# Sub keys folded into the query weights on the chip, and a mixer in three PSUM banks with its SSD branch ahead of the level loop

## Chip, cores and metric

The kernel runs on one core of one Trainium2 chip. The time is device time of one execution in microseconds (us). The core's engines are PE (TensorE, matmuls and transposes, its weight loads shown as PEld), DVE (VectorE), ACT (ScalarE), POOL (GpSimd, which here issues the gathers) and SP (SyncE, which issues most loads); each has a queue of its own and works through it in order. They meet through semaphores. Sixteen DMA engines move the data. PSUM has eight banks of 512 fp32 values in each of 128 partitions.

## What is computed

One block over 1024 tokens of width 1024, in fp32:

```
x   = x + mixer(rmsnorm(x))          # SSD branch (8 heads x 64) and gated DeltaNet, "GDN" (4 heads x 128)
h   = rmsnorm(x) * norm_ffn_w
q   = (h @ w_q)                      # 16 lists (8 heads x 2 halves) of 128
s   = q . sub_keys                   # 16 lists of 128 scores
s1, s2 -> top 16 each -> 50 candidate sums -> top 16 of them   # 128 experts a token
y   = sum_k gate_k * gelu(h . u_tab[id_k]) * v_tab[id_k]
out = rmsnorm(x + y) * norm_final_w
```

The mixer's GDN part needs the inverse of a unit triangular matrix in each tile; the kernel builds it in seven levels (block sizes 1 to 64). Both tables, u and v, have 16384 rows of 4 KB.

## The kernel before

**Stages.** The front stage (`front_stage`, lines 194 on) normalises x, multiplies by w_in, convolves, and stores the results to scratch memory; near its end SyncE loads w_out and w_q, a slice of each (lines 288 and 289) behind each store. The tile stage (`tile_stage`, lines 533 on) takes the 1024 tokens in eight tiles of 128. For a tile it runs the mixer, the query product, and the two selections that give 128 picks for each token; then the expert part gathers a row of u for each of 128 picks (items "U": one gather of 128 rows, 512 KB, and one DVE product against h at L1180) and the rows of v (items "V": one gather for each token and two products on PE at L838).

**Rounds.** The expert part of tile e runs in the same round as the mixer of tile e+1. A round takes the loop body `body(m, e)`: `body(0, None)` is tile 0's mixer with no experts; `body(1, 0)` has tile 0's first half of experts; six full rounds follow, in which the first part interleaves this tile's U items with the previous tile's remaining 60 V items, and the last part is 68 V items; two bodies without a mixer end the program.

**Order.** Every engine's queue is written by the same two lists: the steps of the mixer and scoring (`steps`), and a fixed `SEQUENCE` of expert items. Between steps stands `share()`, and the n-th call emits the items up to `SHARE_ENDS[n-1]`. The calls are at corresponding places on PE, DVE and ACT. In `body(0, None)` share emits nothing. `MARKS` sets the ends: items 16 to 120 over shares 2 to 27 (the mixer and the out-projection), the rest of the U part up to the 42nd share, then the tail. POOL issues gathers in sequence order into a ring of ten slots of 512 KB (L794); a slot is free again when PE or DVE has used it.

**PSUM.** `bank` has four banks for the steps, `h_ps` two (h of the experts' tile), `y_ps` two (the V sums).

**Steps of the mixer on which the change bears.** Row transposes of the 12 heads' logs on PE (L865) into three banks, read by 12 DVE operations (L1262). GDN: key products (L879, L880), then Y, the start of the inverse. The level loop, six turns: PE multiplies by X (L901), ACT copies (L1083), PE makes two sets of products (L907, L908), DVE subtracts them from X and Y (L1306, L1307; the last at L1319) and prepares the next level (L1310). Behind the loop: w (L914), the SSD product with the carried state (L919), v_new (L923, L924), the SSD state update (L930), then on DVE the SSD output and state in seven operations (L1322 to L1333) before the GDN outputs (PE L937 to L939, DVE L1337 on). Out-projection at L956, the sum with x at L1363.

**Scoring.** Eight transposes bring the norm's weights into two banks as a row (L847); DVE multiplies (L1367); h is transposed and multiplied by w_q into four banks (L974). ACT copies q; PE transposes it (L983), ACT copies again (L1129, L1131), PE multiplies by the keys (L987), four times; one ACT copy of 2048 columns (L1135) gives the scores, and DVE's first selection begins at L1219. The picks are ready at L1419.

**Start of the tile stage.** SyncE loads constants (L746), then tile 0's inputs: tok (L755, L756), ch (L757), zgs (L758), x (L761). The first to use them is L1236. PE transposes the sub keys, loaded into a ring slot, at L994.

## Time and profile before

| | us |
|---|---|
| median of 3 runs | 3587.24 (3586.83 to 3588.61) |
| profiled execution, own time | 3575.1 |
| its span in the trace | 3573.5 |
| PE busy | 2597.0 (73%) |
| DVE busy | 2078.7 (58%) |
| POOL busy | 2038.3 (57%) |
| ACT busy | 334.7 (9%) |
| moved by DMA | 1159.13 MB, mean 324 GB/s |

The busy shares are means over stages of different kinds: the front stage up to about 460 us, tile 0's own pass up to about 665, then rounds of some 360 us each, then the last bodies. A stage is read by itself, in stretches and timelines. In a timeline row the number in brackets is the idle time of the engine before that instruction, with what released it. PE's clock has two levels, 1.2 and 2.4 GHz; the profile gives the granted clock as a share of the higher. "Cold" below means the lower one.

### The profile page before, as it was taken

To read this page: it belongs to the slowest core of one execution; us is meant where nothing else is said; L and a number is where in the kernel's file an instruction comes from. 1 tells how busy PE (TensorE), PEld (TensorE's weight loads), DVE (VectorE), ACT (ScalarE), POOL (GpSimd) and SP (SyncE) were. 2 spreads that over 40 slices of the span, in tenths; PEclk is the share of its full clock that TensorE was granted. 3 is DMA by queue.
4 is the path that set the end of the run, shared out by engine and by line. 5 is a ranking of instruction groups with operands and counts; after the bars stand their busy time and mean duration, and the time that the engine had idled before them with its cause. 6 is when DMAs were issued, how large, how long until landed. Compare 5 with 4: busy or idle time off the path is not lost.

```text
span 3573.5 us, 30245 instructions
## 1 busy us (share of the span) xinstructions
PE 2597.0 (73%) x8914; PEld 1022.7 (29%) x8914; DVE 2078.7 (58%) x4579; ACT 334.7 (9%) x705; POOL 2038.3 (57%) x2109
## 2 busy tenths in 40 slices
PE   7999956157857785778578857785778677765588
PEld 4444543143123212321232124212321232110121
DVE  3332032879478647865686567755875586646600
ACT  2221011001001100010001000100110011000000
POOL 1100000346766776677667766775677667777765
PEclk8999978568979997899799979897999789976699
DMA  3334320579999999999999999999999999999998
GB/s 101 106 112 148 132 80 0 208 241 393 352 388 375 409 366 373 375 410 366 369 374 409 368 384 358 410 367 360 377 410 375 373 372 409 362 396 410 409 399 349
DMA packets 351628, 1159.13 MB, mean 324 GB/s; under 512 B 43280, under 2 KB 72848, under 8 KB 350480
## 3 DMA queue, kind: packets, MB, share of 16 engines
q0 software_dynamic: 301024, 1094.89, 79.3%
q1 hardware_dynamic: 46256, 58.69, 4.9%
q10 hardware_dynamic: 4224, 4.35, 0.3%
q14 instruction: 102, 0.84, 0.1%
q8 instruction: 22, 0.36, 0.0%
HBM read 1128.37 MB, written 29.43 MB: 324 GB/s over the span
## 4 chain that ended last, share of the span: by engine, by line
DMA 32%; PE 16%; DVE 15%; issue 14%; POOL 9%; ACT 1%; SPq 0%; POOLq 0%; DVEq 0%; ACTq 0%
DMA ring<-in_peer_v_dram,picks_T 12%; DMA ring<-in_peer_v_dram,at_T 10%; DMA ring<-in_peer_u_dram,picks 9%; DVE ring L1180 9%; POOL ring L794 9%; PE y_psum L838 8%; PE tile_psum L901 1%; PE tile_psum L908 1%; PE tile_psum L974 1%; PE tile_psum L907 1%; DVE arena L1262 1%; PE tile_psum L865 1%; PE tile_psum L956 1%; ACT arena L1083 1%; DVE arena L1306 1%
## 5 line engine op out<-in xcount | busy, mean ns | idle before, releaser
L838 PE MATMUL y_psum<-ring,spread 128*32 128x512 f32 x4096 | 1365.2, 678 | 502.8 <-DMA ring<-in_peer_v_dram,at_T 401.3
L1180 DVE CUSTOM_DVE_ANT_0 ring<-ring,h_psum 128x1024 f32<-128x1024 f32 x1024 | 1224.7, 1219 | 368.1 <-DMA ring<-in_peer_u_dram,picks 321.8
L794 POOL DMA_INDIRECT ring<-in_peer_u_dram,picks x1024 | 965.7, 943 | 803.2 <-DVE picks L1419 314.1
L838 PEld LDWEIGHTS y_psum<-ring,spread 128*32 128x32 f32 x4096 | 279.3, 117 | 1494.6 <-DMA ring<-in_peer_v_dram,at_T 637.3
L794 POOL DMA_INDIRECT ring<-in_peer_v_dram,picks_T x544 | 579.1, 1064 | 196.8 <-issue 130.5
L794 POOL DMA_INDIRECT ring<-in_peer_v_dram,at_T x480 | 452.3, 942 | 202.9 <-issue 121.1
L324 PE MATMUL proj<-hn_T,w_blk 128*128 128x512 f32 x640 | 280.1, 597 | 1.3 <-DVE hn_T L453 1.3
L974 PE MATMUL tile_psum<-w_q,arena 128*128 128x512 f32 x512 | 235.2, 612 | 8.8 <-ACT arena L1119 8.8
L324 PEld LDWEIGHTS proj<-hn_T,w_blk 128*128 128x128 f32 x640 | 121.2, 192 | 146.9 <-issue 145.2
L1444 DVE SCALAR_TENSOR_TENSOR h_psum<-x,stat,h_psum 128x1024 f32<-128x1024 f32 x8 | 10.3, 1290 | 257.0 <-PE h_psum L847 257.0
L974 PEld LDWEIGHTS tile_psum<-w_q,arena 128*128 128x128 f32 x512 | 96.3, 194 | 145.3 <-issue 134.3
L477 DVE TENSOR_SCALAR conv_sum<-pre,taps 128x1024 f32<-128x1024 f32 x20 | 19.0, 951 | 196.6 <-ACT pre L412 196.6
L956 PE MATMUL tile_psum<-w_out,arena 128*128 128x512 f32 x256 | 122.3, 631 | 8.8 <-ACT arena L1108 8.8
L1033 ACT COPY spread<-zero 128x8 f32<-128x8 f32 (+1 forms) x104 | 21.5, 207 | 1069.9 <-PE y_psum L838 954.3
L339 PE MATMUL proj<-w_zgs,w_blk 128*128 128x512 f32 x256 | 111.8, 595 | 3.2 <-ACT pre L412 2.1
L304 POOL DMA_DIRECT2D ch_scr<-post x20 | 11.3, 563 | 174.8 <-ACT post L417 174.8
L1202 DVE COPY arena<-y_psum 128x1024 f32<-128x1024 f32 x8 | 9.8, 1224 | 156.7 <-PE y_psum L838 155.8
L306 POOL DMA_DIRECT2D tok_scr<-frames x20 | 18.4, 921 | 135.9 <-ACT frames L421 128.8
L907 PE MATMUL tile_psum<-arena 128*128 128x128 f32 x320 | 71.1, 307 | 27.0 <-ACT arena L1083 27.0
L901 PE MATMUL tile_psum<-arena 128*128 128x128 f32 x384 | 60.0, 303 | 36.2 <-DVE arena L1306 34.6
L1180 DVE DVE_READ_ACCUMULATOR2_ANT dots<- 128x1 f32 x1024 | 84.8, 83 | 0.0
L908 PE MATMUL tile_psum<-arena 128*128 128x128 f32 x384 | 77.8, 299 | 5.4 <-ACT arena L1083 5.4
(217 smaller groups left out, 2228.9 us busy)
## 6 DMA issues: line engine op xcount, KB each, us to landing
ring<-in_peer_u_dram,picks POOLq DMA_INDIRECT x1024, 7.1
w_blk<-in_w_in_dram SPq DMA_DIRECT2D x20, 512.0 KB, 3.6
ch_scr<-post POOLq DMA_DIRECT2D x20, 512.0 KB, 2.9
tok_scr<-frames POOLq DMA_DIRECT2D x20, 512.0 KB, 3.8
ring<-in_peer_v_dram,picks_T POOLq DMA_INDIRECT x544, 7.3
w_q<-in_peer_w_q_dram SPq DMA_DIRECT2D x8, 1024.0 KB, 6.6
ring<-in_peer_v_dram,at_T POOLq DMA_INDIRECT x480, 7.6
arena<-tok_scr SPq DMA_DIRECT2D x8, 768.0 KB, 9.2
```

The lines of the kernel that those rows point to most:

```text
L324: last = nc.tensor.matmul(proj[j][:, cols], w_blk[:, j, k, :], hn_T[:, k, cols], start=(k == 0), stop=(k == KD - 1))
L339: last = nc.tensor.matmul(out, h_tile[:, j, k, :], w_zgs[:, k, at:at + n], start=(k == 0), stop=(k == KD - 1))
L794: pool.indirect_dma_start(ring[:, j], None, tables[kind], bass.IndirectOffsetOnAxis(ap=at, axis=0)).then_inc(filled[j], 16)
L838: last = nc.tensor.matmul(y_ps[quad * STEPS:(quad + 1) * STEPS, half], lines[:, quad, at:at + STEPS], ring[:, j, half * BANK:(half + 1) * ...
L865: last = nc.tensor.transpose(heads(1 + h // 4)[:, h % 4], logs[:, 0, h:h + 1].broadcast_to([P, P]), ident[:])
L901: last = nc.tensor.matmul(heads(1)[:, h], M_T[:, n % 2, h], X[:, h], start=True, stop=True)
L907: nc.tensor.matmul(heads(2)[:, h], Y[:, h], MX[:, h], start=True, stop=True)
L908: last = nc.tensor.matmul(heads(3)[:, h], MX[:, h], Y[:, h], start=True, stop=True)
L956: last = nc.tensor.matmul(bank[:, 2 + half], mixT[:, k], w_out[:, k, half * BANK:(half + 1) * BANK], start=(k == 0), stop=(k == KD - 1))
L974: last = nc.tensor.matmul(bank[:, b], h_T[:, k], w_q[:, k, b * BANK:(b + 1) * BANK], start=(k == 0), stop=(k == KD - 1))
L1083: nc.scalar.copy(MX, heads(1)).then_inc(s["MX_copied"], 1)
L1180: nc.vector.tensor_tensor_reduce(out=ring[:, j], in0=ring[:, j], in1=h_ps[:], scale=1.0, scalar=0.0, op0=ALU.mult, op1=ALU.add, accum_out= ...
```

## The change

The caller now hands over w_q transposed and cut into 16 lists, and the keys transposed, as plain layouts; no arithmetic is done there. In tile 0's pass the kernel multiplies each list of the query weights by its keys: eight matmuls of 128x128 for a list (an item "W", a fold), into `h_ps` and `y_ps` in turn, which that pass doesn't use otherwise, and one DVE operation that multiplies by the ffn norm's weights and writes 128 columns of w_q. SyncE loads ten lists into the ring's slots ahead of the mixer's inputs and six more as slots come free. The 16 folds are spread over the first 26 shares of `body(0, None)`: 0 in share 1, 1 in 3, 2 in 5, 3 in 6, 4 in 8, 5 in 9 (all before the level loop), 6, 7, 8 and 9 in shares 11, 13, 14 and 16 (the level loop), 10, 11, 12 in 18, 19, 21, then 13 to 15 in 22, 24, 26 (around the out-projection). The front stage no longer loads w_q.

Scores then come from h in one product (32 matmuls of 512 columns as before); ACT scales x by the statistic alone to make h, and copies each bank of scores when it is full. Query copies, transposes and key products, and the row transposes of L847 into `bank`, are gone; four shares fewer are called, and `SEGMENTS` and `MARKS` follow.

The mixer uses three banks. The row transposes come in two parts with a wait for DVE's first four reads between them, and one share stands before them in place of after. The SSD product with the state goes behind the transposes of Y, before the level loop; the SSD state's products into the first turn of the loop behind the product by X, and PE waits there for DVE's SSD operations before the level's other products. DVE does its SSD operations before the loop. ACT's statistic of the SSD output moves into the third turn.

```diff
-SEGMENTS = 63
+SEGMENTS = 59
-MARKS = ((0, 0), (1, PRELUDE), (27, 120), (42, HOLE), (43, SEQUENCE.index(("R", 0, 0)) + 1), (SEGMENTS + 1, len(SEQUENCE)))
+MARKS = ((0, 0), (1, PRELUDE), (27, 120), (38, HOLE), (39, SEQUENCE.index(("R", 0, 0)) + 1), (SEGMENTS + 1, len(SEQUENCE)))
+FOLDS = [("W", l, 0) for l in range(LISTS)]
+FOLD_MARKS = ((0, 0), (26, LISTS), (SEGMENTS + 1, LISTS))
...
-                    sp.dma_start(w_q[:, some], w_q_src[:, some]).then_inc(w_late_loaded, 16)
...
+        SCORE_BANKS = (2, 0, 1, 2)
+        head_row = lambda h: heads(2 if h < 4 else 1)[:, h % 4]
...
             def body(m, e):
+                if e is None:
+                    for l in range(SLOTS):
+                        sp.dma_start(ring[:, l], A["w_q_T"][l]).then_inc(s["wq_first"], 16)
...
                     sp.dma_start(x2[:], rows(x_rows, m)).then_inc(s["x2_in"], 16)
+                if e is None:
+                    for l in range(SLOTS, LISTS):
+                        sp.wait_ge(s["wq_ready"], l - SLOTS + 1)
+                        sp.dma_start(ring[:, l - SLOTS], A["w_q_T"][l]).then_inc(s["wq_rest"], 16)
...
+                if kind == "W":
+                    if n < SLOTS:
+                        pe.wait_ge(s["wq_first"], 16 * SLOTS)
+                    else:
+                        pe.wait_ge(s["wq_rest"], 16 * (LISTS - SLOTS))
+                    if n >= 2:
+                        pe.wait_ge(s["wq_copied"], n - 1)
+                    for k in range(KD):
+                        last = nc.tensor.matmul(folded(n)[:, k], ring[:, n % SLOTS, k * P:(k + 1) * P], keys_T[:, n % 2], start=True, stop=True)
+                    last.then_inc(s["wq_ready"], 1)
...
+                share()
                 pe.wait_ge(s["logs_copied"], m + 1)
-                for h in range(HEADS):
-                    last = nc.tensor.transpose(heads(1 + h // 4)[:, h % 4], logs[:, 0, h:h + 1].broadcast_to([P, P]), ident[:])
+                for h in (*range(SSD_H, HEADS), *range(4)):
+                    last = row_of_head(h)
                 last.then_inc(s["rows_ready"], 1)
-                share()
+                pe.wait_ge(s["decay_gdn"], m + 1)
+                for h in range(4, SSD_H):
+                    last = row_of_head(h)
+                last.then_inc(s["rows_ready"], 1)
...
                 last.then_inc(s["X_turned"], 1)
-                share()
                 pe.wait_ge(s["qk_ready"], m + 1)
+                for g in range(SSD_G):
+                    half = slice(g * SSD_R * SSD_P, (g + 1) * SSD_R * SSD_P)
+                    group = slice(g * SSD_R, (g + 1) * SSD_R)
+                    last = nc.tensor.matmul(bank[:, 2, half], C_T[:, g], S_ssd[:, group].rearrange("p h w -> p (h w)"),
+                                            start=True, stop=True)
+                last.then_inc(s["cs_ready"], 1)
+                share()
...
                     last.then_inc(s["MX_ready"], 1)
+                    if n == 1:
+                        pe.wait_ge(s["y_part"], 2 * m + 1)
+                        pe.wait_ge(s["x_end_ready"], m + 1)
...
+                        last.then_inc(s["bx_ready"], 1)
+                        pe.wait_ge(s["y_part"], 2 * (m + 1))
+                        pe.wait_ge(s["S_ssd_ready"], m + 1)
                     pe.wait_ge(s["MX_copied"], (NL - 1) * m + n)
...
-                pe.wait_ge(s["y_part"], 2 * (m + 1))
+                share()
+                for h in range(GDN_H):
+                    nc.tensor.matmul(heads(1)[:, h], q_ch[:, h], S_gdn[:, h], start=True, stop=True)
                 pe.wait_ge(s["v_new_copied"], m + 1)
...
+                if kind == "W":
+                    dve.wait_ge(s["wq_ready"], n + 1)
+                    tt(w_q[:, :, n * P:(n + 1) * P], folded(n), over_free(w_cols[:, 0], P), ALU.mult).then_inc(s["wq_copied"], 1)
...
+                dve.wait_ge(s["cs_ready"], m + 1)
+                tt(y_ssd, heads(2, SSD_H, SSD_P), over_free(e_in[:, 0:SSD_H], SSD_P), ALU.mult).then_inc(s["y_part"], 1)
+                tt(S_ssd[:], S_ssd[:], over_free(e_all[:, 0:SSD_H], SSD_P), ALU.mult).then_inc(s["S_ssd_part"], 1)
+                dve.wait_ge(s["y_part"], 2 * m + 1)
+                tt(y_ssd, y_ssd, heads(0, SSD_H, SSD_P), ALU.add).then_inc(s["y_part"], 1)
+                dve.wait_ge(s["bx_ready"], m + 1)
+                dve.wait_ge(s["S_ssd_part"], 3 * m + 1)
+                tt(S_ssd[:], S_ssd[:], heads(2, SSD_H, SSD_P), ALU.add).then_inc(s["S_ssd_ready"], 1)
+                tt(y_skip, xs, over_free(d_head[:], SSD_P), ALU.mult).then_inc(s["S_ssd_part"], 1)
...
                 share()
                 for n in range(1, NL):
...
+                act.wait_ge(s["x2_r_ready"], m + 1)
+                nc.scalar.activation(h2, x2[:], ACT.Copy, scale=stat[:, 5:6]).then_inc(s["h2_ready"], 1)
...
                 for b in range(4):
                     share()
-                    act.wait_ge(s["q_ready"], 4 * m + b + 1)
-                    if b < 2:
-                        nc.scalar.copy(q[:, b], square(b)).then_inc(s["q_copied"], 1)
+                    act.wait_ge(s["score_ready"], 4 * m + b + 1)
+                    nc.scalar.copy(score[:, 4 * b:4 * (b + 1)], square(SCORE_BANKS[b])).then_inc(s["score_copied"], 1)
                     share()
```

## Rows read from the trace of the kernel before

**Rows 1.** The page: span and DMA share in 40 slices

```profile
span 3573.5 us, 30245 instructions
...
DMA  3334320579999999999999999999999999999998
```

**Rows 2.** Stretches of a tile round: engines' busy us (count), clock, DMA share, GB/s

```profile
core 0: us, PE busy (x) PEld busy (x) DVE busy (x) ACT busy (x) POOL busy (x), PEclk, DMA share, GB/s
1740.00:1770.00 30.00, 17.29 (x77) 10.76 (x78) 26.89 (x56) 2.79 (x4) 17.28 (x19) 0.73 0.93 338
1770.00:1800.00 30.00, 21.71 (x108) 12.12 (x108) 26.34 (x44) 3.06 (x7) 22.61 (x25) 0.87 1.02 410
1800.00:1840.00 40.00, 25.24 (x144) 15.71 (x144) 31.81 (x55) 4.47 (x12) 22.81 (x25) 0.90 0.89 330
1840.00:1960.00 120.00, 95.07 (x280) 34.45 (x282) 88.56 (x157) 13.92 (x24) 89.96 (x96) 0.90 1.03 409
```

**Rows 3.** Source view of L1219: what VectorE waited for before it (us, times)

```profile
  ACT arena L1135: 43.9, 1
```

**Rows 4.** Timeline, tile 0, query to selection: start, us, instruction [idle <- releaser]

```profile
571.28 30.09 PE L974 MATMUL tile_psum<-w_q,arena 128*128 128x512 f32 x64 [1.10 <-ACT arena L1119]
...
610.56 1.87 ACT L1135 COPY arena<-tile_psum 128x2048 f32<-128x2048 f32 x1 [1.25 <-PE tile_psum L987]
612.57 3.19 DVE L1219 MAX8 arena<-arena 128x8 f32<-128x128 f32 x16 [43.94 <-ACT arena L1135]
...
664.73 1.02 POOL L794 DMA_INDIRECT ring<-in_peer_u_dram,picks  x1 [314.06 <-DVE picks L1419]
```

**Rows 5.** Timeline, start of the tile stage: an issue of SyncE, the first consumer

```profile
468.40 0.78 SPq L755 DMA_DIRECT2D arena<-tok_scr  x1
...
480.45 0.17 DVE L1236 TENSOR_TENSOR small<-arena,head_bias 128x16 f32<-128x16 f32 x1 [2.77 <-DMA arena<-zgs_scr]
```

**Rows 6.** Stretches of the same start, columns as in Rows 2

```profile
468.00:474.00 6.00, 0.00 (x0) 0.00 (x0) 0.00 (x0) 1.28 (x1) 0.00 (x0) 0.50 0.82 186
474.00:480.00 6.00, 0.69 (x2) 0.29 (x2) 0.23 (x2) 0.58 (x2) 0.00 (x0) 0.50 0.99 366
```

**Rows 7.** Timeline, tile 0, eight cold 128x128 matmuls, first and last pair

```profile
494.37 0.80 PE L879 MATMUL tile_psum<-arena 128*128 128x128 f32 x2 [1.16 <-ACT arena L1074]
...
497.52 0.40 PE L880 MATMUL tile_psum<-arena 128*128 128x128 f32 x2
```

**Rows 8.** Timeline, tile 0, eight warm 128x128 matmuls, their reader, the next matmuls

```profile
503.86 0.49 PE L907 MATMUL tile_psum<-arena 128*128 128x128 f32 x2 [0.67 <-ACT arena L1083]
...
505.95 0.69 DVE L1306 TENSOR_TENSOR arena<-arena,tile_psum 128x512 f32<-128x512 f32 x1 [2.85 <-PE tile_psum L908]
...
506.78 1.13 PE L901 MATMUL tile_psum<-arena 128*128 128x128 f32 x8 [0.87 <-DVE arena L1306]
```

**Rows 9.** Timeline, tile 0, VectorE over 1024 columns of PSUM

```profile
564.35 1.22 DVE L1363 TENSOR_TENSOR x<-x,tile_psum 128x1024 f32<-128x1024 f32 x1 [18.97 <-PE tile_psum L956]
```

**Rows 10.** Timeline, tile 0, behind the level loop

```profile
533.16 1.03 PE L930 MATMUL tile_psum<-arena 128*128 128x256 f32 x4
...
534.23 0.69 DVE L1322 TENSOR_TENSOR arena<-tile_psum,exps 128x512 f32<-128x512 f32 x1 [4.85 <-PE tile_psum L930]
```

**Rows 11.** Timeline, a full round, the first reader of the row transposes

```profile
1743.49 3.19 DVE L1262 SCALAR_TENSOR_TENSOR arena<-tile_psum,logs,floor 128x128 f32<-128x128 f32 x12 [2.73 <-PE tile_psum L865]
```

**Rows 12.** Timeline, a full round, before and in the first level

```profile
1778.88 3.56 PE L838 MATMUL y_psum<-ring,spread 128*32 128x512 f32 x8
...
1786.40 0.68 DVE L1306 TENSOR_TENSOR arena<-arena,tile_psum 128x512 f32<-128x512 f32 x1
```

**Rows 13.** Timeline, a full round, behind the level loop

```profile
1820.63 0.69 DVE L1322 TENSOR_TENSOR arena<-tile_psum,exps 128x512 f32<-128x512 f32 x1 [6.88 <-PE tile_psum L930]
...
1825.19 0.94 POOL L794 DMA_INDIRECT ring<-in_peer_v_dram,at_T  x1 [3.81 <-DVE dots L1180]
...
1831.94 0.68 DVE L1337 TENSOR_TENSOR arena<-tile_psum,exps 128x512 f32<-128x512 f32 x1
```

More of the change, by code:

```diff
@@ L1487 @@
     arrays, args = {}, {}
-    for name, value in {**inputs, **constants()}.items():
+    keys, w_q = inputs.pop("peer_sub_keys"), inputs.pop("peer_w_q")
+    laid_out = {"keys_T": _np.asarray(keys)[0].transpose(2, 0, 1),
+                "w_q_T": _np.asarray(w_q)[0].T.reshape(LISTS, P, D)}
+    for name, value in {**inputs, **laid_out, **constants()}.items():
         a = _np.ascontiguousarray(value)
```

189 lines of the change are left out of this document (77 added, 112 removed).

## The prediction

> **What bounds the kernel now.** I read the page first, then stretches, then two timelines. The page gives a DMA share of 9 (90% or more) in nearly every slice from the tenth on [rows 1]: the rounds that gather expert rows run at the pace of the DMA engines. The stretches of one full round say how closely. While it does its out-projection, query product and key scores the DMA share is 1.03 at 409 GB/s [rows 2], so work taken out there buys nothing. Of the round's mixer only two stretches of the mixer fall below 410: 30 us at 338 GB/s, worth 30 x (1 - 338/410) = 5.3 us, and 40 us at 330, worth 7.8 us [rows 2]. The 30 us between them, around the first levels, lose nothing. So a round has some 13 us in its mixer that the change could win, and the six full rounds with a mixer and tile 1's round have it.
>
> Tile 0 is different. Nothing is gathered until its picks exist: POOL's first gather starts at 664.73 after 314 us of idleness behind DVE's L1419 [rows 4]. Each microsecond added to or taken from tile 0's own pass moves everything behind it, one for one.
>
> **Scoring (removed: query copies, transposes, key products).** In tile 0 the query product ends at 571.28 + 30.09 = 601.37 and the first selection starts at 612.57 [rows 4], 11.2 us later. The new kernel copies each bank as it is filled, so behind the last product stands one copy of 512 columns: a quarter of L1135's 1.87 us [rows 4] and a start of its own, 0.7 us. Tile 0: -10.5 us. In the other seven tiles L1219 never waited for the scores: its one wait for L1135, 43.9 us, is tile 0's [rows 3]. There the same removal is worth 0; its cover is the gather stream at 409 GB/s, and even if the four shares fewer (six items to a share instead of four or five) upset that, the items are the same. The eight row transposes and the multiplication by the norm's row go too; the scaling goes from DVE to ACT, one 1024-column pass for another, behind the same statistic: 0, at most a few tenths in tile 0.
>
> **Weights loaded in tile 0, ahead of the mixer's inputs.** SyncE now issues ten loads of 512 KB, 5.24 MB, between the constants and L755, which was issued at 468.40; its data were first used at 480.45 [rows 5]. The engines moved 186 GB/s in the first half of that and 366 GB/s in the second [rows 6]. At 366 GB/s 5.24 MB take 14.3 us. Pauses in the first half can hide some, at 0.82 share 1 us [rows 6], and the megabyte of query weights that the front stage no longer loads last makes room too. Bounds 5 and 16 us, taken: +12.5. Fold 0 lies in that wait and is free. The six later loads go out behind the mixer's own and are due only at fold 10: 0.
> The Trainium skill (DMA: Bandwidth & Descriptors, section on queues, rings and completion order) says that on each DMA engine the descriptors of one issuer's queue are consumed in ring order, which speaks against putting 5 MB ahead of the mixer's inputs. By it they pay the whole 14.3 us less pauses; if the engines shared themselves out among the transfers of a queue instead, the inputs, which are fewer bytes, could be in some 8 us sooner than that. No row here has such a pair side by side.
>
> **The folds.** Each of 16 is eight 128x128 matmuls on PE and a 1024-column DVE multiplication out of PSUM. Eight such matmuls, warm: from 503.86 to their reader at 505.95, 2.09 us [rows 8]; cold, 494.37 to 497.92, 3.55 us [rows 7]. DVE: 1.22 us [rows 9]. Both sit in the shares of tile 0, which are in the same places on both engines. In the level loop PE's fold comes behind the level's products and DVE's ahead of the subtraction that the next level needs. So PE's 2.09 and DVE's 1.22 stand one behind the other on the chain: 3.3 us, with nothing taken off, since PE's gap of 0.87 us [rows 8] was DVE's subtraction, which is now later. Four folds fall in the level loop: 13.2. Folds 1 to 5 lie before it, two of them probably cold; serial they would be 2 x 4.8 + 3 x 3.3 = 19.5 us, of which I take a third off for ACT copies and DVE products that run beside them: 13. Behind the loop folds 10 and 15 are serial again (DVE waits for a fold that PE does behind the signal which it needs next): 6.6; fold 11 costs DVE's 1.2, fold 12 half, fold 13 about 1.1 behind the copy of mixT, fold 14 PE's 2.1: 5. Sum 38 us (13.2 + 13 + 11.6). Bounds: with DVE's part all hidden and PE's gaps filled 16 x (2.09 - 0.87) = 19.5; with all serial and two cold 15 x 3.3 + 3 = 52.5. The value stands near the middle because the order in both queues is fixed.
>
> **The SSD branch moved.** In tile 0 DVE waited 4.85 us for L930 before L1322 [rows 10]. Behind the loop that wait, PE's L930 (1.03 us) and four DVE operations go; a shorter wait for the GDN products stays: -3.1. Before level 2 PE gets two groups of about 1 us and a wait for DVE's state update, DVE its seven operations of 0.69: +1.5. Net -1.6.
> In a full round the same exchange has larger ends. Behind the loop DVE idled 6.88 us until 1820.63, and POOL in turn had waited 3.81 us for a slot from DVE at 1825.19; the GDN operations started at 1831.94 [rows 13]. From the end of its last level at 1820.63 - 6.88 = 1813.75 to there are 18.2 us: the wait, seven operations of 0.6 to 0.7 (4.5), and two shares of gathers' products that take the other 6.8. Of it the shares and one small operation stay, 7.3; an estimate of PE's chain to the GDN products (it no longer holds L930, still waits for ACT twice) makes that 8.7. So -9.5. Before the loop DVE gets a wait for the first group (an estimate: PE's transposes and one group of the kind of L930, 1.9), a wait for the second, which PE reaches only behind a share that took 3.56 us [rows 12] (3.6), and its operations (4.2): DVE, which was at level 2 at 1786.40 [rows 12], gets there some 9.6 later if PE is cold, 8 if warm. The two nearly cancel. What decides is that the stretch before the loop had DMA to spare and the one behind it had none [rows 2]: a hole of this size is covered in part by the ten slots. I take -1.5 a round; bounds +5 (the hole opens and the old one doesn't close) and -7.8 (the whole shortfall at 330 GB/s goes).
> The row transposes in two parts: the last eight heads' readers waited 2.73 us [rows 11] for all twelve; with eight transposes ahead of the first signal it is about 0.8 less, and PE's share fills a wait it had. The new wait, for DVE's first four reads, holds four transposes and a share of PE: a microsecond. Taken -1.2 a round, between +1 and -3. A full round: -2.7, six: -16. Tile 1's round gathers for its first half only and its chain is bare of the second's matmuls, so PE arrives early: an estimate with tile 0's waits and the shares' products left in gives -9 behind the loop, +5.7 before it and -0.7 for the transposes: -4.
> Banks: three instead of four make no wait beside those named.
>
> **The sum.** Tile 0: 12.5 + 38 - 10.5 - 1.6 = +38.4. Rounds: -20. Together +18.4 on a span of 3573.5. The profiled execution took 3575.1 us and the median of the runs is 3587.24, 12.1 more; I carry the difference over unchanged: 3587.2 + 18.4 = 3605.6, say 3606.
>
> **Rivals.**
> (1) Not slower: the hole behind the loop closes and the new one stays covered. Place: 1800 to 1840 of each round. For it: POOL's 3.81 us [rows 13] and a full DMA share before the loop [rows 2]. Against: the chain from there on is no shorter by my count. Price: six times -(7.8 + 1.5) and -9 for tile 1, -65; it decides once rounds give more than 38 us, 5.5 each. Time 3587 + 38.4 - 65 = 3561.
> (2) The folds are cheap: PE and DVE overlap, 19.5 in place of 38. For it: PE idles in much of tile 0's mixer. Against: the fixed order. Time 3587.
> (3) The new hole isn't covered: DVE waits for the second group behind PE's cold share in each round and the old shortfall stays, +4 a round in place of -2.7, nothing at tile 1. Time 3587 + 38.4 + 24 = 3650.
> (4) The ten loads do not hold the mixer's inputs back: +4 for 12.5. Time 3597. It is the other half of the queue rule above.
>
> **How the numbers follow.** Forecast 0.50, (1) 0.17, (2) 0.17, (3) 0.11, (4) 0.05. A measurement here can tell 0.2%, 7 us. The forecast's own range is 3594 to 3624 from the bounds of loads and folds, which are unlikely to be at one end together. For 8 in 10 the range must reach near (1) and some way to (3): 3566 to 3640. Faster by over 0.2%: (1) and a part of (2), 0.21. Within: most of (2), 0.16. Slower: 0.63.
>
> **What would show it.** Tile 0: the first read of L1236's successor at about 493 instead of 480.45; a level with a fold some 3.3 us longer than one without; the selection within 1 us of the last query product; POOL's first gather at 703 (664.73 + 38). A start of gathering before 690 means that the folds were overpriced. Rounds: from one h_psum product to the next 3 us less than before; the idleness before L1322 gone, and a new one before the state's addition; the stretch behind the loop at 350 GB/s or so. If that stretch shows 400, rival (1) holds; if the stretch before the loop falls to 350, rival (3). The stretches with query products must stay at 409; if they fall, the reasoning on hidden work is wrong.

## The result and the profile after

The changed kernel takes 3669.14 us (median of 4 runs, 3660.93 to 3674.08) against 3587.93 for the kernel before beside it: a ratio of 1.0223, 95% interval 1.0204 to 1.0242. Slower, as forecast, but by 81 us instead of 18, outside the range. The profiled execution took 3666.01 us, its span is 3664.4. The page of the changed kernel, the lines that answer to [rows 1]:

```profile
span 3664.4 us, 29822 instructions
...
PE 2615.3 (71%) x8720; PEld 1023.1 (28%) x8720; DVE 2094.9 (57%) x4587; ACT 310.3 (8%) x672; POOL 2051.6 (56%) x2109
```

Every engine has about the work that it had (PE, DVE and POOL are busy 13 to 18 us longer in all); the rest of the 91 us of span is waiting. The medians are 81 us apart, the spans 91, since the profiled execution of the kernel before ran 12 us under its median and that of the changed kernel 3. Where the 91 arise shows when both traces are cut at the same instructions of VectorE (DVE). The start of the product that leaves h in PSUM ends one round and begins the next. From one to the next (us):

```
                tile 0 ends   tile 1's   six full rounds, mean
before             665.2       318.9       361.2
changed            704.9       313.1       370.8
                   +39.7        -5.8        +9.6  (x 6 = +57)
```

Tile 0 and tile 1 came as forecast (+38.4, -4). The full rounds did not: -2.7 forecast, +9.6 found. That is the error.

**Tile 0, step by step.** DVE's starts, counted from its memset of the GDN state at the start of the tile stage ("the memset" below): to the first use of the mixer's inputs 16.8 us before and 29.3 now (+12.5, forecast 12.5); from there to the loop's first mask +12.4 (13); to level 2 +5.4 and through the levels +11.9 (together 14.7); from the last level to the out-projection's sum +6.8 (8.5); to the first selection -10.6 (-10.5). The start and one level with a fold, in the changed kernel's timeline:

```profile
470.67 5.70 SPq L756 DMA_DIRECT2D ring<-in_w_q_T_dram  x10
...
494.07 0.18 DVE L1247 TENSOR_TENSOR small<-arena,head_bias 128x16 f32<-128x16 f32 x1 [0.32 <-DMA arena<-zgs_scr]
...
534.19 1.95 PE L823 MATMUL y_psum<-keys_T,ring 128*128 128x128 f32 x16
...
536.18 1.23 DVE L1185 TENSOR_TENSOR w_q<-y_psum,w_cols 128x1024 f32<-128x1024 f32 x1
537.32 0.68 DVE L1335 TENSOR_TENSOR arena<-arena,tile_psum 128x512 f32<-128x512 f32 x1
...
538.14 1.13 PE L936 MATMUL tile_psum<-arena 128*128 128x128 f32 x8 [2.00 <-DVE arena L1335]
```

The first reader of the inputs starts at 494.07 where it started at 480.45 [rows 5]. The fold's matmuls, DVE's product and then the subtraction stand one behind the other, 1.95 + 1.2 us ahead of the reader that the level waits for. The end of the pass, in the same timeline:

```profile
621.71 29.62 PE L1010 MATMUL tile_psum<-w_q,arena 128*128 128x512 f32 x64 [1.10 <-ACT arena L1141]
...
652.10 1.06 DVE L1230 MAX8 arena<-arena 128x8 f32<-128x128 f32 x5 [36.44 <-ACT arena L1146]
```

Behind the last query product (621.71 + 29.62 = 651.33) the first selection comes at 652.10, 0.77 us later, forecast 0.7 [rows 4].

**A full round.** The timeline of the changed kernel around the first level, in the round from 1758.61:

```profile
1832.28 0.69 DVE L1314 TENSOR_TENSOR arena<-ident_m,arena 128x512 f32<-128x512 f32 x1
...
1835.13 0.69 DVE L1317 TENSOR_TENSOR arena<-tile_psum,exps 128x512 f32<-128x512 f32 x1 [1.56 <-PE tile_psum L928]
...
1840.38 0.69 DVE L1323 TENSOR_TENSOR S_ssd<-S_ssd,tile_psum 128x512 f32<-128x512 f32 x1 [3.37 <-PE tile_psum L944]
...
1845.07 0.94 POOL L806 DMA_INDIRECT ring<-in_peer_v_dram,at_T  x1 [7.55 <-DVE dots L1191]
...
1850.49 0.68 DVE L1335 TENSOR_TENSOR arena<-arena,tile_psum 128x512 f32<-128x512 f32 x1
...
1851.23 2.08 PE L936 MATMUL tile_psum<-arena 128*128 128x128 f32 x8 [8.03 <-DVE arena L1335]
...
1857.80 0.69 DVE L1335 TENSOR_TENSOR arena<-arena,tile_psum 128x512 f32<-128x512 f32 x1 [4.16 <-PE tile_psum L954]
...
1860.42 0.94 POOL L806 DMA_INDIRECT ring<-in_peer_u_dram,picks  x1 [4.45 <-PE y_psum L860]
```

From the identity's subtraction to level 2 DVE needs 18.2 us here (9.5 before, [rows 12]): both new waits are there, and the one for the second group is 3.37. PE then waits 8.03 us and comes back slower, its eight matmuls take 2.08 us where eight warm ones take 1.16 (same line, 1859.55), and from its next products at 1853.98 to their reader at 1857.80 it takes 3.82 where 2.09 were enough in tile 0 [rows 8]. The granted clock is 0.52 from 1851 to 1858, the lower of the two levels, and 1.00 from 1858 to 1870; the kernel before had 1.00 from 1782 to 1789, around its level 2. What the prediction didn't price are the two rows of POOL: 7.55 and 4.45 us in which no gather goes out. The stretches of that round, beside [rows 2]:

```profile
1824.00:1838.00 14.00, 10.56 (x27) 3.44 (x26) 9.42 (x16) 0.59 (x1) 10.48 (x11) 0.65 1.02 404
1838.00:1854.00 16.00, 6.37 (x39) 5.24 (x37) 13.15 (x22) 1.25 (x4) 6.79 (x8) 0.80 0.70 241
1854.00:1894.00 40.00, 30.43 (x184) 21.77 (x184) 31.60 (x53) 4.98 (x14) 22.96 (x25) 0.91 0.90 315
1894.00:2014.00 120.00, 92.67 (x224) 28.10 (x224) 86.79 (x147) 9.99 (x19) 90.27 (x96) 0.89 1.03 410
```

Ahead of level 2 there are now 241 GB/s where 410 were; through and behind it 315, not better than the 330 of before; out-projection and query product are at 410 as they were.

### The profile page after: what moved, and what is told of

It reads as the page before. It is cut to its first block, busy times and chain, and to the rows that moved or that the text cites. A ratio compares the mean times of both kernels' runs of the same rounds, so it can differ in the third digit from the quotient of the medians.

```text
span 3664.4 us, 29822 instructions
## 1 busy us (share of the span) xinstructions
PE 2615.3 (71%) x8720; PEld 1023.1 (28%) x8720; DVE 2094.9 (57%) x4587; ACT 310.3 (8%) x672; POOL 2051.6 (56%) x2109
## 4 chain that ended last, share of the span: by engine, by line
DMA 32%; issue 16%; PE 15%; DVE 13%; POOL 10%; ACT 1%; SPq 0%; POOLq 0%; DVEq 0%
DMA ring<-in_peer_v_dram,at_T 11%; DMA ring<-in_peer_v_dram,picks_T 11%; POOL ring L806 10%; DMA ring<-in_peer_u_dram,picks 10%; PE y_psum L860 8%; DVE ring L1191 7%; PE tile_psum L936 1%; PE tile_psum L954 1%; PE tile_psum L953 1%; PE tile_psum L1010 1%; DVE arena L1276 1%; DVE arena L1335 0%; ACT arena L1103 0%; DMA arena<-zgs_scr 0%; PE y_psum L833 0%
## 5 line engine op out<-in xcount | busy, mean ns | idle before, releaser
L860 PE MATMUL y_psum<-ring,spread 128*32 128x512 f32 x4096 | 1397.7, 689 | 559.3 <-DMA ring<-in_peer_v_dram,at_T 449.4
L806 POOL DMA_INDIRECT ring<-in_peer_v_dram,picks_T x544 | 587.7, 1080 | 199.1 <-issue 131.7
L936 PE MATMUL tile_psum<-arena 128*128 128x128 f32 x384 | 65.5, 323 | 86.9 <-DVE arena L1335 86.9
L953 PE MATMUL tile_psum<-arena 128*128 128x128 f32 x320 | 77.7, 331 | 28.8 <-ACT arena L1103 21.6
L954 PE MATMUL tile_psum<-arena 128*128 128x128 f32 x384 | 87.3, 329 | 5.4 <-ACT arena L1103 5.4
L936 PEld LDWEIGHTS tile_psum<-arena 128*128 128x128 f32 x384 | 56.2, 224 | 107.9 <-DVE arena L1335 71.0
```

Source lines behind the costliest of these rows:

```text
L806: pool.indirect_dma_start(ring[:, j], None, tables[kind], bass.IndirectOffsetOnAxis(ap=at, axis=0)).then_inc(filled[j], 16)
L860: last = nc.tensor.matmul(y_ps[quad * STEPS:(quad + 1) * STEPS, half], lines[:, quad, at:at + STEPS], ring[:, j, half * BANK:(half + 1) * ...
L936: last = nc.tensor.matmul(heads(1)[:, h], M_T[:, n % 2, h], X[:, h], start=True, stop=True)
L953: nc.tensor.matmul(heads(2)[:, h], Y[:, h], MX[:, h], start=True, stop=True)
L954: last = nc.tensor.matmul(heads(0)[:, h], MX[:, h], Y[:, h], start=True, stop=True)
```

## Experiments

Chips of two kinds appear below. Where the two kernels above were measured, and on the chip of the half rows, the kernel before has medians of 3583 to 3588 us: the faster chips. All other runs were made on four other chips, where its medians are 3940 to 3978 us and its runs scatter by half a per cent and more: the slower chips. A full round lasts 404 to 413 us in every kernel run there; no trace of the kernel before was taken on them. Tile 0 gathers nothing, so its times are compared across all chips; rounds only within one kind. Rows of one execution show where the slower chips lose time (what the copy of mixT waited for, in us and times; this is the changed kernel there):

```profile
L1128 ACT COPY arena<-tile_psum x8: 1012/1012/1012, 598.1 to 3231.2; 128x1024 f32<-128x1024 f32 x8
its engine sat idle before it (us, times) until:
  remote: 65.5, 5
```

In the changed kernel's trace on a faster chip all eight of these copies followed PE's transposes directly; here five of them wait for something that the profile can't name, with PE's out-projection behind them. DVE has such waits ahead of level 2 (8.07 us in one row of the spread kernel below), and POOL has them too: of the waits that the profile calls "remote" this execution has 42 on ACT, 20 on DVE and 107 on POOL, where none of the six traces from faster chips has one. These stalls hide much of what the change does to the rounds.

### Half rows: what sets a round's pace

Each gather reads 2 KB instead of 4 KB for every pick. All instructions of the engines stay; half of every expert product is left out (the other half of the slots is zero), and a pick's number now names a half row, so the rows read are others than the experts'. The edit is in four kernels: before, changed, folds and scoring with the mixer of before, and the changed kernel with a spread SSD branch (below).

```
-  pool.indirect_dma_start(ring[:, j], None, tables[kind],
+  pool.indirect_dma_start(ring[:, j, 0:BANK], None, tables[kind].rearrange("e (two d) -> (e two) d", two=2),
```

> The kernel before, but each gather of an expert row reads half a row (2 KB instead of 4 KB, the other half of each slot is set to zero once), so that the gathers can't set a round's pace. Left out: half of every expert product. All engine instructions stay. Its round is the bare chain of engines; it is the base for the next three. Expected: rounds of 290 to 330 us, in which the stage from the identity's subtraction to level 2 is some 9.5 us and the stage from the last subtraction to the GDN output some 18 us.

> The changed kernel with half rows. The prediction held that the two holes of a full round nearly cancel on the engines' chain (+8 to +9.6 ahead of the loop, -9.5 behind it), and that the DMA slack covers what is left. If they cancel, rounds from small operands to the out-projection's sum are within 3 us of the first of these kernels, and the +9.5 us of the real kernel come from how the gathers' slots meet the hole. If PE's idleness ahead of level 2 costs the chain more by itself (cold levels, expert products pushed into the out-projection), the chain is 6 to 10 us a round longer here too.

> Folds, new scoring and new shares with the mixer of before, with half rows. It tells the shares' new places and the scoring from the mixer: if the scoring's smaller work shows when no gather covers it, the round is 10 to 20 us shorter than that of the first of these kernels, all of it behind the out-projection; in the mixer's stages it equals the first within 1 us.

> The changed kernel with the spread SSD branch (three banks) and half rows. If the cost of the branch ahead of the loop is DVE's wait for the second group and its seven operations ahead of its share, the stage to level 2 takes some 12 us instead of some 17, and the levels 1 to 3 us more for the operations spread over them, so the mixer is 2 to 4 us shorter than the changed kernel's. If total work alone counts, it is equal.

Measured: 3458.1, 3529.95, 3511.07 and 3497.32 us (two runs each, at most 6.2 us apart), beside 3583.06 for the kernel before. The first is the surprise: half the bytes take 3.5% off, and its rounds last 345.6 us where 290 to 330 were expected. Nor did the scoring show as 10 to 20 us less: the third kernel's round is 1.0 us longer. And the change costs 3529.95/3458.1 = 1.0208, almost the 1.0223 of full rows. Means of six full rounds from the timelines, cut at DVE's instructions; the last line is the time that POOL was idle beyond its usual 0.30 us between two gathers:

```
                            full rows          half rows
                          before changed   before changed old mixer spread
to the loop's first mask   70.7   72.2      59.9   61.4    61.9    61.3
the identity's subtraction  0.7    0.7       0.7    0.7     0.7     0.7
 from there to level 2     10.1   17.8       9.8   17.6    10.0    11.6
levels                     26.5   29.4      27.7   29.1    26.6    31.1
 last level to GDN output  18.2   11.0      18.0    8.8    18.1     8.5
to mix's last part         12.9   13.7      12.8   13.0    12.8    13.0
to the sum of the out-p.   29.9   32.6      28.1   32.3    28.4    32.1
to the first selection     77.3   73.3      74.7   71.4    71.0    71.4
to the next round         114.9  120.1     113.9  117.1   117.0   117.6
round                     361.2  370.8     345.6  351.4   346.6   347.3
POOL idle in it            32.0   39.9      11.5   17.4    12.9    12.9
```

Round less POOL's idleness is 329 and 331 us with full rows and 334 in all four with half rows: a full round has 256 gathers, and POOL issues one every 1.24 us or more. In the stretch of query product and scores of a round, half rows, first the engines with POOL (columns as in [rows 2]), then POOL alone:

```profile
1808.00:1928.00 120.00, 96.54 (x319) 34.62 (x318) 82.90 (x187) 14.55 (x29) 90.70 (x97) 0.96 0.72 210
...
1857.20 0.95 POOL L797 DMA_INDIRECT ring<-in_peer_u_dram,picks  x1 [0.30 <-issue]
1858.46 0.95 POOL L797 DMA_INDIRECT ring<-in_peer_u_dram,picks  x1 [0.30 <-issue]
1859.71 0.95 POOL L797 DMA_INDIRECT ring<-in_peer_u_dram,picks  x1 [0.30 <-issue]
```

97 gathers in 120 us, as with full rows (96 in the changed kernel's stretch above), and 210 GB/s is about half of 410, at a DMA share of 0.72. So 410 GB/s is, within some per cent, also the rate at which POOL asks for rows: 524288 bytes in 1.24 us are 423 GB/s. The prediction read the DMA share of 1.03 as the DMA engines' limit alone and took missing GB/s for slack that a ring of ten slots covers. The profile's 56% for busy POOL hides it, because the 0.30 us behind each issue isn't counted and tile 0 is. The Trainium skill (Perfetto Trace Analysis, "What DMA-bound means") names among the things that can bind a DMA-bound kernel the DMA engines and the issuing engine's sequencer, whose track is then solid with DMA slices. In this trace POOL's track isn't solid even where it never pauses (90.70 us of 120), so it takes the half rows to tell the two apart; with full rows both limits are close.

With POOL as the measure the sum closes: the changed kernel's round is 5.8 us longer with half rows, POOL's idleness 5.9. By stage, half rows, before and changed: ahead of level 2 0 and 3.6 (it waits for DVE's dots), in the levels 1.0 and 6.5 (for PE's expert products), behind the last level 6.0 and 2.0, from there to the next round 0.8 and 0.2; the rest is ahead of the loop's first mask, 3.7 and 5.1. With full rows the same five are 0 and 6.5, 3.4 and 6.4, 6.0 and 3.1, 10.1 and 9.6, 12.5 and 14.2.

The spread kernel parts these terms. Its stage to level 2 is 6.0 us shorter than the changed kernel's, POOL doesn't idle there any more, and its round is 4.1 us shorter; in the levels POOL still idles 6.5, behind the last one 1.4. So the hole ahead of level 2 is the dear part of the mixer, and what is lost in the levels (+5.5) is about what the closed hole behind them gives back (-4.0 to -4.6). In the changed kernel PE is busy for 8.7 of the 17.6 us ahead of level 2 and does two tokens' expert products; in the kernel before it was busy for 15.2 of the 18.0 us behind the last level and did five to six tokens'. A reason why closing that hole gave so little is that PE had gone on freeing slots in it; no run shows this by itself. Of DVE's 9.2 us 4.2 go again in the out-projection's stage, where it now waits 9.6 us for rows instead of 6.0 while POOL issues without pause.

Old mixer against before: +1.0 us, all inside shifts between stages (-3.7 in the scoring, +3.1 in the selection behind it: the shares moved, the items are the same). So shares and scoring cost 1 us, the mixer 4.8 of the 5.8. Single rounds of one kernel lie 2 to 5 us apart here, so the 5.8 and the spread kernel's 4.1 stand out of the means of six, the 1.0 hardly. With full rows the whole is 9.6, and POOL's idleness grows by 7.9, of which 6.5 lie ahead of level 2; no run splits the full rows' loss by part of the change.

### Parts of the change alone

Folds and new scoring with the mixer of before (PE's third share stays ahead of the row transposes, since DVE's third waits for its fold), and the mixer alone with a fourth bank:

```
-  for h in (*range(SSD_H, HEADS), *range(4)):      (first kernel: one group again, SSD branch behind the loop)
+  for h in range(HEADS):
...
-  bank = ps("tile_psum", [P, 3, BANK])             (second kernel: scoring, weights and shares of before)
+  bank = ps("tile_psum", [P, 4, BANK])
```

> Folds, the ten loads and the new scoring as in the changed kernel; the mixer as before: four PSUM banks, the SSD branch behind the level loop, all twelve row transposes in one group. Only PE's third share stands ahead of the row transposes, as in the changed kernel, since the folds in the shares need that. Theory M (the six full rounds lose 9.5 us each through the SSD branch ahead of the loop): the rounds from one h_psum product to the next are back at 361 to 362 us, tile 0 keeps its +40, and the time is 3587 + 40 = 3627 us (3620 to 3633). Rival F (the rounds lose through the new marks of the shares and the scoring): rounds stay at 370 to 372, time 3670 to 3680.

> The other half alone: weights, query copies, transposes, key products and share marks as before; the SSD branch ahead of the level loop, the row transposes in two parts, each reader in the bank that the changed kernel gives it (a fourth bank exists, the out-projection still goes to banks 2 and 3). Theory M: full rounds of 370 to 372 us, tile 1's round 6 less than before, tile 0 1 to 2 less: 3587 - 2 - 6 + 57 = 3636 us (3628 to 3644). Rival F: rounds of 361, time near 3580.

> The changed kernel with one edit: PE's share that stood between the first group (C with the state) and the level's first product now stands behind the second group (B with x). In the changed kernel DVE waited 3.37 us for that second group, behind eight expert products of 3.27 us. If DVE's wait for the second group is a fair part of the new hole, DVE is some 2.4 us earlier at level 2 and each full round is 1.5 to 2.4 us shorter: 3655 to 3660 us. If the hole is the sum of DVE's added operations ahead of its share and PE's idleness behind them, PE gets to the level's last product at the same time as before the edit and little changes: within 4 us of 3669.

> The first of these kernels (folds and new scoring, SSD branch behind the loop) with the row transposes in two parts, DVE's subtractions of the GDN heads first. This prices that part alone. The prediction had -1.2 us a full round between +1 and -3: 3627 - 7 = 3620 us against 3627 for the first one. If the stretch has DMA slots to spare before the loop, the part is worth nothing (within 3 us of the first); if the added wait counts, up to 6 us more.

> The changed kernel itself, beside the kernel before on the chip of these runs, whose gathers land later than in the first pair of profiles (rounds of some 410 us instead of 361). Tile 0's pass must end at 704.9 within a microsecond or two, since it gathers nothing. If the 9.5 us a full round come from the engines' order and the DMA engines have slots to spare here, the ratio is again near 1.02; if gathering itself is slower than the new hole, the hole is covered, rounds are those of the other kernels here, 410 us, and only tile 0's 39 less tile 1's 6 stays: a ratio of 1.005 to 1.01.

All on slower chips, so the expected absolute times can't be judged, only ratios to the kernel before beside them: 1.0040 (1.0011 to 1.0070), 0.9986 (0.9952 to 1.0020), 0.9977 (0.9947 to 1.0006), 1.0050 (1.0012 to 1.0087); the changed kernel itself 1.0006 (0.9975 to 1.0037). The 2.2% of the faster chips aren't there, though tile 0's pass is as long (710.4 us, 249.0 from the memset): something behind it must give it back. The first two were run once more:

> Folds, loads and new scoring with the mixer of before (the kernel of the first experiment again), on a chip where the kernel before takes 3583 to 3588 us as in the first pair of profiles. Theory: the mixer costs the full rounds most of their 9.5 us. With half rows this kernel's round was 1.0 us longer than that of before and the changed kernel's 5.8 longer. Expected: full rounds of 361 to 364 us, tile 0 42 to 50 us longer, 3587 + 46 + 10 = 3643 us at most and 3630 at least, 26 to 40 below the changed kernel. Rival (shares and scoring cost the rounds, not the mixer): rounds of 368 and more, 3670 to 3680.

> The other half alone, again: scoring, weights and shares as before, the mixer as changed but with a fourth bank. Theory: full rounds of 367 to 371 us, tile 0 and tile 1's round 5 to 8 us less together: 3587 - 6 + 6 x 8 = 3629 us (3615 to 3640). Rival: rounds of 361 to 363, 3582 to 3592.

Again a slower chip: 1.0003 (0.9967 to 1.0038) and 0.9966 (0.9940 to 0.9993). As tests of the full rounds these four failed; the half rows did it. What they tell: tile 0's end is 711.3 with folds and the old mixer, 666.9 with the new mixer alone (202.8 us from the memset, 201.7 in its second run, against 201.6), so tile 0's loss is the folds' and loads'. The share moved behind the second group changes nothing in tile 1's round (16.7 us to level 2, 16.9 in the changed kernel), where that share has no expert products. In the full rounds it does: DVE's wait for the second group is 0.1 to 1.6 us instead of 2.3 to 3.4, and the stage takes 15.7 to 17.2 us, in one round with a stall of the chip 21.3, against 17.9 to 18.8. So that wait is some 2 us of the hole; what 2 us less are worth on a faster chip wasn't measured. The rows in two parts: from h's product to the loop's first mask 71.7 us a round with and without them, worth nothing here.

One difference does show. From the out-projection's sum to the first selection tile 1's round takes 61.8 to 62.4 us in the kernels with the new scoring on slower chips and 75.1 to 79.1 in those with the old; on a faster chip it was 50.9 and 52.5. The old scoring hands over between PE and ACT with nine copies, the new one with four, and on those chips ACT starts late. I take this for a reason why the changed kernel costs nothing there; no run isolates it.

### Loads and folds

```
-  for l in range(SLOTS): sp.dma_start(ring[:, l], A["w_q_T"][l])      (ahead of tile 0's inputs; now behind them)
-  FOLD_MARKS = ((0, 0), (26, LISTS), (SEGMENTS + 1, LISTS))
+  FOLD_MARKS = ((0, 0), (4, 0), (26, LISTS), (SEGMENTS + 1, LISTS))
...
-  items, ends = ... (FOLDS, FOLD_ENDS)                                (second kernel: DVE has lag = 1)
+  items, ends = ... (FOLDS, [0] * lag + FOLD_ENDS)
```

> The changed kernel with SyncE's ten loads of the query weights issued behind tile 0's inputs for the mixer instead of ahead of them, and no fold in the first four shares, so that no engine waits for a load in front of its own mixer work. This prices the load term of the prediction (+12.5 us, bounds 5 and 16). If the ten loads held the inputs back one for one, the first use of the inputs comes some 12 us sooner, at about 482, and tile 0's pass ends at about 692 instead of 704.9. If the engines share themselves out among the queue's transfers whatever the order (rival 4's half of the rule), the first use is within 4 us of 494 and the end within 5 us of 704.9.

> The changed kernel with DVE one share behind PE in the folds: each of DVE's 16 multiplications stands one share later, so that it copies a fold that PE finished a share ago. This prices the serial order that the prediction charged with 3.3 us a fold. If PE's 1.95 and DVE's 1.22 us stand one behind the other on the chain, that overlap takes 1.2 to 2 us off each of some 12 folds: tile 0's pass ends 14 to 24 us sooner than 704.9, at 681 to 691. If PE alone sets the pace (DVE's part was hidden already), the end moves by less than 5 us.

The first kernel also has no fold in the first four shares. Both are single executions, so only their timelines are used. The timeline with the inputs first:

```profile
473.68 6.73 SPq L769 DMA_DIRECT2D ring<-in_w_q_T_dram  x10
480.02 0.17 DVE L1246 TENSOR_TENSOR small<-arena,head_bias 128x16 f32<-128x16 f32 x1 [1.77 <-DMA arena<-zgs_scr]
...
494.06 3.78 PE L822 MATMUL y_psum<-keys_T,ring 128*128 128x128 f32 x16 [1.88 <-DMA ring<-in_w_q_T_dram]
```

The first use is back at 480.02: the loads ahead of them had held the inputs back by 14 us (13.4 from the memset), so rival (4) is wrong and the step right. That the folds' place moved too doesn't matter for it: in the changed kernel this instruction waits last for its own input (0.32 us, zgs_scr). It is what the rule of the Trainium skill that the prediction named gives (DMA: Bandwidth & Descriptors, section on queues, rings and completion order); the trace agrees. The end of the pass is at 232.3 us from the memset, with DVE one share behind PE at 226.0. What that gains depends on the execution of the changed kernel that it is held against. From 240.1 us (the trace above) it is 7.8 and 14.1; from 249.0 (the same kernel on a slower chip, as these two are) it is 16.7 and 23.0. So a fold costs 0.9 to 1.4 us less than the serial 3.3 that I charged when DVE copies what PE finished a share ago, and whether the loads' 12.5 us reach the end whole stays open. Fold 0 still waits 1.88 us for its load, and the folds crowd into later shares.

The difference between the two values doesn't follow the kind of chip: tile 0's pass with all folds took 240 us in one execution and 247 to 250 in others, on both. Five of these us are in the level loop (34.6 and 39.6 us), where the granted clock was 0.87 in the short one and 0.80 in the long ones. The kernel before has such a scatter too, 201.6 us above and 207.8 with half rows.

### The SSD branch spread, and all three together

DVE does only the two operations that free bank 0 ahead of its share; decay, addition, skip and gate of the state and of y go to turns 2 to 4. In three banks the group B with x stands in the loop's last turn, when bank 2 is free, and the skip product goes where G was:

```
-  if n == 1:
+  if n == NL - 1:
       pe.wait_ge(s["x_end_ready"], m + 1)
       ...
-  dve.wait_ge(s["bx_ready"], m + 1)        (ahead of the loop)
+  if n == 2: tt(S_ssd[:], S_ssd[:], over_free(e_all[:, 0:SSD_H], SSD_P), ALU.mult)
+  ...
+  dve.wait_ge(s["bx_ready"], m + 1)        (behind the last subtraction)
```

> Scoring and weights as before, four PSUM banks, and the SSD branch ahead of the loop in another form: both of its product groups (C with the state, B with x) stand behind one another ahead of the first level, the second in the fourth bank; DVE does only the two operations that free bank 0 (scaling and adding to y) ahead of its share, and spreads the five others over turns 2 to 4 of the loop. Theory: the new hole was 8.7 us because DVE waited for the second group and did seven operations ahead of its share, with PE idle and cold behind them. Here DVE goes from the end of the identity's subtraction to level 2 in 11 us instead of 18.2, while the stretch behind the loop stays at some 11 us instead of 18: each full round is shorter than before by up to 5 us where the mixer sets the pace, 3587 - 30 = 3557 us on the first chip, a ratio of 0.990 to 0.998 here. Rival: what matters is PE's and DVE's total work ahead of the level loop's end, wherever it stands: a ratio of 1.00.

> The changed kernel with the spread SSD branch alone (three banks, weight loads and folds as changed). In tile 0 the spread branch takes the chain of waits that stood ahead of level 2 away: of the 33 us that the kernel with all three edits gained at the end of tile 0's pass, 22 to 25 were expected of the loads and folds; if the remaining 8 to 11 are the spread branch's, tile 0's pass ends here at 694 to 697. If they come from the folds and the branch meeting (a fold in a turn in which DVE still did the branch), it ends within 4 us of 704.9. From the end of the identity's subtraction to level 2 tile 1's round should take 12.4 us instead of 17.0.

> The changed kernel with three edits: tile 0's inputs ahead of the ten weight loads and no fold in the first four shares; DVE one share behind PE in the folds; the SSD branch spread in three banks (B with x in the last turn of the loop, when bank 2 is free, DVE's remaining operations in turns 2 to 4 and behind the last subtraction). Single, the first two ended tile 0's pass 8.5 and 16.6 us sooner than the changed kernel's 704.9. If the load term and the serial folds add up, it ends at 680 to 684, 16 us behind the kernel before; if both took the same time off the chain, at 688. Against the changed kernel the time falls by these 22 us and by what the rounds give back: 0 where gathers set the pace, 9 to 12 us each where the mixer does.

> The changed kernel with inputs ahead of the weight loads, DVE one share behind PE in the folds, and the spread SSD branch in three banks, again. Tile 0 5 to 7 us longer than before, tile 1's round 8 to 12 shorter, full rounds 1.7 us longer by the engines' chain with half rows, up to 5 with the gathers' slots: 3587 + 6 - 10 + 6 x (1.7 to 5) = 3593 to 3613 us, 55 to 75 below the changed kernel.

> Scoring and weights of before with the spread SSD branch in four banks, again. Tile 0 4 us shorter than before, tile 1's round 6 to 10 shorter; full rounds: the stage to level 2 +2, the levels +3, the stage behind the loop -8, the out-projection's stage +2 to +4: within 2 us of 361. 3587 - 4 - 8 + 0 = 3575 us (3563 to 3590). If the out-projection's stage grows by 4 and the gathers' slots add theirs, 3595.

On slower chips: spread with the old scoring 0.9999 (0.9973 to 1.0025) and, once more, 0.9952 (0.9921 to 0.9984); spread in the changed kernel 0.9967 (0.9940 to 0.9994), its tile 0 243.5 us from the memset, between the changed kernel's two values; all three edits 0.9891 (0.9856 to 0.9926) and 0.9855 (0.9783 to 0.9926), against the changed kernel beside the first of these 3899.39/3944.27 = 0.9886, with no run of one as long as the shortest of the other. That is clear of noise, though under 2%. The first gather of the first run with all three edits, to be held against 664.73 [rows 4] and 704.44 in the changed kernel:

```profile
671.38 1.03 POOL L805 DMA_INDIRECT ring<-in_peer_u_dram,picks  x1 [319.18 <-DVE picks L1434]
```

So it beats both kernels on the slower chips. Tile 0's pass takes 206.9 us (205.3 in the second run), 5 more than before and 33 or 42 less than the changed kernel's two values. From the longer one the two single edits had given 39.7 together, from the shorter 21.9, so it isn't shown that they gain more together than alone. With all three the level loop takes 24.9 us, 22.7 before. On a faster chip it wasn't run. There the half rows speak for its mixer: 347.3 us a round against 351.4, the stage to level 2 is 11.6 instead of 17.6, though PE's lateness in the levels (POOL idle 6.5) stays. An estimate from those rows, tile 0 +5, tile 1's round some -8 (301.5 against 309.8, half rows), six rounds between +1.7 and +5: between 3594 and 3614 us, no gain on the kernel before.

## Why the prediction was right or wrong

- **The bound, wrong.** The full DMA share was right as a reading, and the stretches with query products kept their 410. But the limit behind it was POOL's issuing as much as the engines' bytes, and it has no slack to catch up: with full rows POOL idles 0.8 us in the 107 us from mix's last part to the first selection. What POOL loses in the mixer is lost to the round. The prediction also says that the stretch before the loop "had DMA to spare" and the one behind it none; [rows 2] show a share of 1.02 before the loop, none to spare, and 0.89 behind it.
- **Loads, right.** +12.5 forecast and found. **Folds, right:** 38 forecast, and the stages give 12.4 + 5.4 + 11.9 + 6.8 = 36.5 in this execution, the mixer's part in it included (forecast -1.6; alone it left the pass at 201.7 to 202.8 us, +0.1 to +1.2). Against the 249.0 us of the changed kernel's other trace they would be some 45. Rival (2), cheap folds, is false for this order. **Scoring, right:** -10.6 in tile 0 and, with the shares, no gain in a full round (+1.0 with half rows).
- **Tile 1's round:** -5.8, forecast -4.
- **Full rounds, wrong: the term "-1.5 a round" for the SSD branch.** Its parts on DVE were good: ahead of level 2 +7.7 (8 to 9.6), behind the loop -7.2 (-9.5) with full rows, -9.2 with half. The step that failed is the next one, "a hole of this size is covered in part by the ten slots", with "the two nearly cancel". They nearly cancel on DVE (+7.8 and -9.2) and not on POOL: with half rows 3.6 us of its idleness opened ahead of level 2 and 5.5 in the levels, and 4.0 closed behind them; with full rows 6.5 and 3.0, and 2.9. Taking 6.0 of the 7.8 us ahead of level 2 away gave 4.1 of the mixer's 4.8 us back, so the ten slots had not covered it. The bound of +5 was too low as well, and rival (3), this mechanism, was priced at +4 with chance 0.11, where the mixer's part is 4.8 with half rows and up to 8.6 with full.
- **What no term held:** levels that are longer behind the hole (+2.9; in the round above the lower clock of the first one accounts for 2.7: 2.08 for 1.16 and 3.82 for 2.09 us), and the row split, taken at -1.2: the stage to the first mask grew by 1.5 (full and half rows alike; the old mixer with the new shares has 2.0), so that is the shares', and a gain of the split can't be seen.

## What to carry to other kernels

Where one engine issues all gathers, take the round apart as its issuing time plus its waits, and price each hole by what it makes that engine wait, not by the length of the hole on the engine that shows it. Two holes of like size on one consumer need not have one price: here 6 us of the hole ahead of level 2 were worth 4.1 us a round, while closing 9 us behind the levels gave the issuing engine 4.0 us back against 5.5 that it lost within them. To learn whether bytes or issues set the pace, halve the bytes and leave the instructions.

## What the runs showed of the hardware

- Half the bytes of 1.1 GB of gathers took only 3.5% off; the usual interval of POOL's issues stayed at 1.24 to 1.25 us, with 2 KB rows as with 4 KB.
- The same program had medians of 3583 to 3588 us on some chips and 3940 to 3978 on four others. The traces from the slower ones have 168 to 190 waits each, on POOL (98 to 118), ACT and DVE, for which the profile names no releaser but "remote"; the six from faster ones have none. They stand at the same places in most rounds: DVE's ahead of level 2 in the spread kernel is there in each of the six full rounds, 6.8 to 9.1 us. What they are stays open.
- Tile 0's level loop took 34.6 or 39.6 us with the same instructions, at granted clocks of 0.87 and 0.80.
